# Up-projections of a split-precision transformer kernel with 512 moving columns per matmul, their result read from two half banks by ScalarE and VectorE

## What is computed

```
first block, twice per layer:
  a, b = split(rmsnorm(x, g) @ w_up, 2)          # w_up 1024 x 5632
  x = x + 0.5 * (silu(a) * b) @ w_down           # w_down 2816 x 1024
second block, once per layer:
  a, b = split(dwconv3(rmsnorm(x, g) @ w_up), 2)
  x = x + (silu(a) * b) @ w_down
```

## Time and profile before

| what | value |
|---|---|
| median of 3 runs | 2204.83 us (2196.54 to 2207.15) |
| the profiled execution, its own time | 2198.97 us |
| its span in the trace | 2197.2 us |
| PE busy | 2062.6 us, 94% of the span |
| DVE busy | 1531.2 us, 70% |
| ACT busy | 1044.9 us, 48% |
| mean granted TensorE clock | 0.981 |

### The profile page before, as it was taken

How to read it: one execution, slowest core, us unless ns; L and a number is a source line. 1 busy time by engine, 2 the same in 40 slices (tenths; PEclk the granted TensorE clock), 3 DMA queues, 4 the chain that set the end, 5 groups by cost and what they waited for, 6 DMA issues and landing times.

```text
span 2197.2 us, 39058 instructions
## 1 busy us (share of the span) xinstructions
PE 2062.6 (94%) x15972; PEld 1949.6 (89%) x15972; DVE 1531.2 (70%) x2165; ACT 1044.9 (48%) x1357; POOL 0.2 (0%) x4
## 2 busy tenths in 40 slices
PE   6999999999999899999998999996999997999998
PEld 6998987788999899989778899996788997778998
DVE  5556888977755665568899676556658776647777
ACT  4444453465544444444426654443455554445554
POOL 0000000000000000000000000000000000000000
PEclk9999999999999999999999999998999998999999
DMA  5555443324655345544332255452225543315544
GB/s 224 184 190 199 157 151 115 116 68 136 220 190 186 141 172 189 199 157 171 135 123 85 87 198 200 172 196 77 77 97 186 187 172 120 106 39 191 192 172 153
DMA packets 51153, 336.68 MB, mean 153 GB/s; under 512 B 5688, under 2 KB 5688, under 8 KB 14696
## 3 DMA queue, kind: packets, MB, share of 16 engines
q1 hardware_dynamic: 50616, 332.72, 43.4%
q10 hardware_dynamic: 432, 2.46, 0.3%
HBM read 334.11 MB, written 1.05 MB: 153 GB/s over the span
## 4 chain that ended last, share of the span: by engine, by line
PE 73%; DVE 16%; ACT 7%; DMA 2%; issue 2%; DVEq 0%; ACTq 0%; SPq 0%
PE bank L367 23%; PE bank L368 22%; PE bank L369 22%; DVE lo L1249 5%; ACT hi L828 3%; DVE cv L1466 2%; DMA raw<-in_w 2%; PE bank L393 1%; PE bank L506 1%; PE bank L514 1%; PE bank L501 1%; DVE qn L1392 1%; PE bank L530 1%; DVE p_sb L1445 1%; DVE rstd L1262 0%
## 5 line engine op out<-in xcount | busy, mean ns | idle before, releaser
L1249 DVE TENSOR_TENSOR lo<-raw,hi 128x2048 fp32r<-128x2048 f32 (+1 forms) x344 | 721.0, 2096 | 318.9 <-ACT hi L828 318.7
L828 ACT ACTIVATE hi<-raw 128x2048 fp32r<-128x2048 f32 (+1 forms) x344 | 601.8, 1753 | 163.7 <-PE bank L369 125.9
L367 PE MATMUL bank<-n_hi,hi 128*128 128x256 f32 x2112 | 599.4, 284 | 41.0 <-DVE n_lo L1253 34.0
L368 PE MATMUL bank<-n_lo,hi 128*128 128x256 f32 x2112 | 596.9, 283 | 0.0
L369 PE MATMUL bank<-n_hi,lo 128*128 128x256 f32 x2112 | 596.8, 283 | 0.0
L367 PEld LDWEIGHTS bank<-n_hi,hi 128*128 128x128 f32 x2112 | 400.3, 190 | 43.5 <-issue 29.5
L367 PE MATMUL bank<-h_hi,hi 128*128 128x256 f32 x1296 | 384.0, 296 | 28.5 <-DVE h_lo L1253 27.0
L368 PEld LDWEIGHTS bank<-n_lo,hi 128*128 128x128 f32 x2112 | 400.3, 190 | 0.2
L369 PEld LDWEIGHTS bank<-n_hi,lo 128*128 128x128 f32 x2112 | 400.2, 189 | 0.0
L368 PE MATMUL bank<-h_lo,hi 128*128 128x256 f32 x1296 | 372.3, 287 | 0.0
L369 PE MATMUL bank<-h_hi,lo 128*128 128x256 f32 x1296 | 372.0, 287 | 0.0
(11 more groups left out here) (209 smaller groups left out, 2326.9 us busy)
## 6 DMA issues: line engine op xcount, KB each, us to landing
raw<-in_w SPq DMA_DIRECT2D x282, 1024.0 KB, 4.8
raw<-in_w SPq DMA_DIRECT2D x62, 512.0 KB, 3.8
bv<-in_bv SPq DMA_DIRECT2D x2, 768.0 KB
x<-in_x ACTq DMA_DIRECT2D x1, 1024.0 KB, 5.0
mask_in<-in_const SPq DMA_DIRECT2D x2, 512.0 KB
out_x<-x SPq DMA_DIRECT2D x1, 1024.0 KB, 3.9
const<-in_const ACTq DMA_DIRECT2D x1, 791.5 KB, 12.7
prm_all<-in_prm ACTq DMA_DIRECT2D x1, 588.0 KB, 8.7
```

The lines of the kernel that those rows point to most:

```text
L367: mm(out, w_hi, a_hi, start=start, stop=False, skip_group_check=True)
L368: mm(out, w_hi, a_lo, start=False, stop=False, skip_group_check=True)
L828: fn(hi[:, s, 0:w], raw[:, s, 0:w], ACT.Copy).then_inc(sem["hi"], 1)
L1249: v.tensor_tensor(lo[:, s, 0:w], raw[:, s, 0:w], hi[:, s, 0:w].bitcast(F32), ALU.subtract)\
```

## The change

Input high and low parts become one tensor `n_both`, and the first two matmuls of a product become one with 512 moving columns, its result over a whole bank: columns 0 to 255 get high by high, columns 256 to 511 high by low. The third matmul (low weight by high input, 256 columns) adds to columns 256 to 511. So each j has a bank of its own, four banks for the up chunks (3, 4 and 6, 7), and the down chunks move to banks 5, 0, 1, 2. The two halves must be added: ACT copies both upper halves to `spill_t`, 512 elements (new semaphore `spill`), DVE adds them to the lower halves (`sum_t`), waits for itself, and multiplies by `rstd`. In ACT's order `spill` stands ahead of what used to wait for `up`, which in the loops is behind a `split`. Nothing else of the orders changes; down chunks and all products of the mixers stay as they are.

```diff
+DOWN_BANKS = (5, 0, 1, 2)
+UP_BANKS = ((3, 4), (6, 7))
...
-    n_hi = sb("n_hi", [P, KT, S], F32R, at_u)
-    n_lo = sb("n_lo", [P, KT, S], F32R, at_u + KT * S * 4)
+    n_both = sb("n_both", [P, 2, KT, S], F32R, at_u)
+    n_hi, n_lo = n_both[:, 0, :, :], n_both[:, 1, :, :]
...
+    def up_banks(u):
+        return psum[:, UP_BANKS[u][0]:UP_BANKS[u][1] + 1, :]
...
+        def up_pair(c, u, ready=None, stat_after=None):
+            take("lo")
+            for k in range(KT):
...
                 for j in range(2):
-                    last = mm3(out[:, j * S:(j + 1) * S], tile(hi, c, 2 * k + j), tile(lo, c, 2 * k + j),
-                               a_hi[:, k0 + k, :], a_lo[:, k0 + k, :], start=start and k == 0 and j == 0)
+                    out = bank[UP_BANKS[u][j]]
+                    mm(out[:, :], tile(hi, c, 2 * k + j), n_both[:, :, k, :], start=(k == 0), stop=False,
+                       skip_group_check=True)
+                    last = mm(out[:, S:2 * S], tile(lo, c, 2 * k + j), n_hi[:, k, :], start=False, stop=True,
+                              skip_group_check=True)
             last.then_inc(sem["pe"], 1)
...
+        def spill(u, c):
+            act.wait_ge(sem["pe"], c)
+            fn(spill_t[:, :, :], up_banks(u)[:, :, S:2 * S], ACT.Copy).then_inc(sem["spill"], 1)
...
                 split(cb + 4)
+                spill(0, i * 3 + after0)
                 tap0(0, at(0))
                 hidden(1)
                 split(cb + 5)
                 silu2(0)
                 split(cb + 6)
+                spill(1, i * 3 + (after0 + 1))
                 tap0(1, at(1))
...
-        def up(u, c, out):
-            v.wait_ge(sem["pe"], c)
-            v.tensor_tensor(out, two(bank[u][:, :]), rstd[:, 0, :].unsqueeze(1).broadcast_to([P, 2, S]), ALU.mult)\
+        def up(u, out):
+            take("spill")
+            link(v.tensor_tensor(sum_t[:, :, :], up_banks(u)[:, :, 0:S], spill_t[:, :, :], ALU.add))
+            v.tensor_tensor(out, sum_t[:, :, :], rstd[:, 0, :].unsqueeze(1).broadcast_to([P, 2, S]), ALU.mult)\
                 .then_inc(sem["up"], 1)
```

More of the change, by code:

```diff
@@ L163, in leave @@
             self.n[k] = before.get(k, 0) + v * times
-_FFN_LOOP = dict(hi=3, lo=3, pe=3, slot=3, load0=16, load1=16, load2=16, half=1, up=2, silu=2, prod=2,
+_FFN_LOOP = dict(hi=3, lo=3, pe=3, slot=3, load0=16, load1=16, load2=16, half=1, spill=2, up=2, silu=2, prod=2,
                  hidhi=2, hid=2)
-PER_FFN1 = dict(_FFN_LOOP)
-PER_FFN2 = dict(_FFN_LOOP, tap0=2, conv3=2, link=2)
+PER_FFN1 = dict(_FFN_LOOP, link=2)
+PER_FFN2 = dict(_FFN_LOOP, tap0=2, conv3=2, link=4)
 def _stream(chunks):
@@ L179, in _ffns @@
 def _ffns(n):
-    return dict(half=n * (PAIRS - 1), up=n * JT, silu=n * JT, prod=n * JT, hidhi=n * JT, hid=n * JT,
+    return dict(half=n * (PAIRS - 1), up=n * JT, spill=n * JT, silu=n * JT, prod=n * JT, hidhi=n * JT, hid=n * JT,
                 dpair=3 * n, ssum=n)
@@ L201 @@
              "ythi", "yth", "conv", "mu", "cc", "csq", "cvar", "cstd", "cn", "cs", "cshi", "csh",
-             "mix", "mixhi", "mixh", "link", "out", "nat", "up", "tap0", "dpair", "mask", "conv3", "es", "uhi", "uh", "ghi", "g",
+             "mix", "mixhi", "mixh", "link", "out", "nat", "spill", "up", "tap0", "dpair", "mask", "conv3", "es", "uhi", "uh", "ghi", "g",
              "fhi", "f", "ssum", "rd", "pn", "yc", "yf", "fsq", "fstat", "fstd", "ysum", "ystd", "yn", "mf", "ya")
@@ L297, in build @@
     assert at_u + 28672 <= at_t
-    bank = [nc.alloc_psum_tensor(f"bank{i}", [P, 512], F32) for i in range(8)]
+    psum = nc.alloc_psum_tensor("bank", [P, 8, 512], F32)
+    bank = [psum[:, i, :] for i in range(8)]
     ident = const[:, C["ident"]:C["ident"] + P]
@@ L375, in tile, with pairs @@
             return part[:, c % SLOTS, i * P:i * P + n]
-        def pairs(c, out, k0, nk, a_hi, a_lo, start, ready=None, stat_after=None):
+        def pairs(c, out, k0, nk, a_hi, a_lo, start, ready=None):
             take("lo")
             for k in range(nk):
+                if ready and k % 2 == 0:
+                    take(ready)
+                for j in range(2):
+                    last = mm3(out[:, j * S:(j + 1) * S], tile(hi, c, 2 * k + j), tile(lo, c, 2 * k + j),
+                               a_hi[:, k0 + k, :], a_lo[:, k0 + k, :], start=start and k == 0 and j == 0)
+            last.then_inc(sem["pe"], 1)
+        def up_pair(c, u, ready=None, stat_after=None):
+            take("lo")
+            for k in range(KT):
                 if k == stat_after:
@@ L407, in summed_stat @@
             pe.wait_ge(sem["const"], 16)
[L408 removed]
+            mm(bank[5][:, 0:S], ones, xsq[:, 0, :], start=True, stop=True).then_inc(sem["stat"], 1)
         def down_tile(c, k, m, h_hi, h_lo, start=False):
[L411 removed]
+            return mm3(bank[DOWN_BANKS[m // 2]][:, (m % 2) * S:(m % 2 + 1) * S], tile(hi, c, 8 * k + m),
                        tile(lo, c, 8 * k + m), h_hi[:, k, :], h_lo[:, k, :], start=start)
@@ L443, in two_tiles @@
                 take("up")
-                pairs(cb + 2, bank[0], 0, KT, n_hi, n_lo, True)
+                up_pair(cb + 2, 0)
                 if early:
@@ L447, in two_tiles @@
                 take("up")
-                pairs(cb + (4 if early else 3), bank[1], 0, KT, n_hi, n_lo, True)
+                up_pair(cb + (4 if early else 3), 1)
                 if not early:
                     down(cb + 4, first)
-            pairs(cb, bank[0], 0, KT, n_hi, n_lo, True, ready="h")
-            pairs(cb + 1, bank[1], 0, KT, n_hi, n_lo, True, stat_after=2)
+            up_pair(cb, 0, ready="h")
+            up_pair(cb + 1, 1, stat_after=2)
             cnt.up("sq", 4)
@@ L816, in act_program @@
         cnt = Count(dict(pe=SLOTS))
+        start = {}
         fn = nc.scalar.activation
@@ L866, in scaled_std, with pe_after @@
             take("stat")
-            fn(std[:, 0, :], bank[7][:, 0:S], ACT.Sqrt, scale=1.0 / D, bias=eps).then_inc(sem["std"], 1)
+            fn(std[:, 0, :], bank[5][:, 0:S], ACT.Sqrt, scale=1.0 / D, bias=eps).then_inc(sem["std"], 1)
         def silu(u, gate_of):
             fn(silu_t[:, u, :], gate_of[:, u, 0, :], ACT.Silu).then_inc(sem["silu"], 1)
+        def pe_after(c):
+            return start["pe"] + c + 1
+        def spill(u, c):
+            act.wait_ge(sem["pe"], c)
+            fn(spill_t[:, :, :], up_banks(u)[:, :, S:2 * S], ACT.Copy).then_inc(sem["spill"], 1)
         def silu1(u):
@@ L886, in ffn1 @@
             scaled_std()
+            spill(0, pe_after(cb))
             silu1(0)
@@ L890, in ffn1 @@
             hidden(0)
+            spill(1, pe_after(cb + 1))
             silu1(1)
@@ L903, in ffn1 @@
                 split(cb + 6)
+                spill(1, i * 3 + (after0 + 2))
                 silu1(1)
@@ L910, in ffn1 @@
             split(c + 2)
+            spill(0, pe_after(c))
             silu1(0)
@@ L913, in ffn1 @@
             split(c + 3)
+            spill(1, pe_after(c + 1))
             silu1(1)
@@ L1005, in layer1 @@
         def layer1():
+            start["pe"] = cnt.at("pe")
             take("prm")
```

40 lines of the change are left out of this document (21 added, 19 removed).

## The result

| | before | changed |
|---|---|---|
| median of the runs, us | 2203.52 (4 runs) | 2224.86 (2222.76 to 2226.78, 4 runs) |
| profiled execution / its span, us | 2198.97 / 2197.2 | 2226.37 / 2224.6 |
| mean granted clock of that span | 0.981 | 0.975 |

A forecast was written before the change was run, and what follows sets the result against it. It took PE, busy 94% of the span, as the bound, with DVE and ACT deciding at starts, ends and in the second block's loop. -3.3 + 15.6 = +12.3 us on 2198.97 gave 2211.3, as median 2217 us, range 2200 to 2230.

The forecast's parts named there:

- 10.9 ns a product: Up-projections on PE: a product falls from 356.1 to 345.2 ns, -23.0 us in all if nothing else holds PE.
- Rival (d): Up-projection matmuls: cost is per column, a 512-column one takes 237.4 ns beside a 256-column one; 2228 us, chance 0.12.
- the -3.3 forecast there: First block's four feed-forward parts: cheaper products less new waits at starts and ends, -3.3 us for the four.
- One of the forecast's own signs of being wrong: First block's feed-forward (`ffn1`): an up chunk above 5.6 us would show the forecast wrong.
- 17.08 us a round, so PE's gain there is nothing: Second block's 18 loop rounds: DVE and ACT set 17.08 us a round, against 17.09 before and 16.74 of PE.
- The circle: Second block's loop: DVE and ACT wait on each other in a closed chain without PE, 17.08 us a round.
- a second register link: DVE between the convolution's halves in the second block's loop: half of 0.11 us extra, twice a round.
- the branch: ACT in the second block's loop: the loop's branch adds 0.15 us, 0.48 instead of 0.33 between two starts.
- rival (b): Part of the gain arrives: mixed stream saves more, 2204 us, or links and branches cost less, 2211; chance 0.19.
- +7.8 a part: Second block: each part's last down chunk starts 7.8 us later, +15.6 us for both parts.
- I price that difference at 0: Second block's end: slower clock after the longer 6.3 us wait counted as 0, upper bound some 3 us a part.
- my case: The main forecast for the whole kernel, 2217 us, own range 2209 to 2226, chance 0.46.

The follow-up runs named there:

- e2: Against the changed kernel: three 256-column matmuls per product again, into the two half banks, with copy and sum kept; 2227.01 us, ratio to before 1.0120.
- e3: Against the changed kernel: wide matmuls kept, copy and sum removed, so up-projections' low-part products are left out of the result; 2193.59 us, ratio to before 0.9958.
- e4: Against the changed kernel: the change only in the first block's four feed-forward parts, second block as before; 2205.43 us, ratio to before 1.0014.
- e5: Against the changed kernel: both 512-column matmuls of a k step first, then both 256-column ones; 2218.83 us, ratio to before 1.0067.
- e1: Against the changed kernel: input laid out so the 512 moving columns are one contiguous run; 2220.82 us, ratio to before 1.0085.

## Why the prediction was right, and where it was not

**Direction and mechanism: right.** It said that the gain per product is eaten by a longer chain at starts and ends, where PE already waits, and most of all in the second block. e2 and e3 show just that, and e4 that the second block holds most of the loss. The sizes of these waits were near: 4.38 us for the second tile (4.9 forecast), the first down chunk 4.3 us later (4.6), the `last_lo` wait 1.2 in the first block (1.5) and 5.2 and 4.9 in the second (6.3).

**"10.9 ns a product": more than twice what came.** It is 4.9 by the rounds. The step that failed is taking 226.5 ns from the value projection and setting it beside 118.7 from the old up chunk: steps of two streams do not carry over into a mixed third. Rival (d) asked just this, with all 10.9 lost. Over the 1408 products of the first block the miss is 8.4 us, and it accounts for most of the distance between the -3.3 forecast there and the +6.1 in the profile. It is also the largest miss in the total, which came out 9.0 us over the forecast difference. One of the forecast's own signs of being wrong came with it: an up chunk of `ffn1` takes (16.93 - 5.70) / 2 = 5.62 us, above 5.6. The Trainium skill's "TensorE: Matmul & The Clock Gate", section "Back-to-back issue gap", gives, in its formula for the isolated gap, about 2.5 ns a matmul beside its columns, so by it a join would save 2.5; the runs show 4.9, nearer to the page than to the 10.9 of my rows; the most that any run showed is 7.4 (e5).

**"17.08 us a round, so PE's gain there is nothing": wrong in the sum, near in its effect.** The circle is 16.85. Of the 0.23 us, 0.11 is the price set on a second register link, which does not show (the half round with the link fits without it); 0.08 is the branch (0.40 us between `silu` and the weight copy at 1789.42, where 0.48 was taken from the earlier trace rows), and the rest rounding in the terms. Its price lay in rival (b). But with PE at 16.93, not 16.74, circle and PE are nearly equal, and 0.16 us a round is all that arrives: 1.4 us a part. PE was not seen waiting before every down chunk, as the forecast had it.

**"+7.8 a part" in the second block.** At the last down chunk of the first part it is 5.4: 1.3 from the faster rounds and 1.1 from the shorter end wait. The first part is 5.6 us longer and the second 9.8. That the sum is 15.3 against 15.6 is luck: chain and rounds cost less than forecast, and some 4 us of clock, which I had priced at 0, fill the gap, nearly all of them in the second part; the windows behind its waits have 0.72 and 0.66.

**"I price that difference at 0": wrong, by some 5 us in the parts.** I looked mainly at the end of a part, where a low stretch was there already, and bounded it by 3 us a part. New stretches came behind new or longer waits at the starts, and the one behind the wait for the first down chunk's low weight was not hidden. Whether the clock also cost time in stages that the change does not touch is not shown: the 6.1 us there are within what single executions scatter by. The time ends at 2224.9, inside my case's own range of 2209 to 2226, but by two errors of one sign, product and clock, and one of the other, the second block's circle and end wait, which were set too long.

## What to carry to other kernels

Joining matmuls saves only what the mixed stream saves: time the stream itself, in a round, before you multiply by a thousand products. A longer evacuation chain costs nothing in the middle of a loop where its engine has room, and its full length at each start and end where PE already waits, so split such a change by place and keep it only where no one waits. What PE loses at a start is not made good in rounds in which PE works without a gap, except by what the rounds themselves became shorter.

## What was not expected of the hardware

Each 0.001 of mean granted clock goes with 1.6 to 2.1 us of this kernel's time, within runs of one program. With wide matmuls on top of the same chain the mean clock was 0.004 lower in the changed kernel and 0.001 lower in e1 than in e2, four runs each, so whether they lower it is open. And 512-column matmuls take 226.5 ns in one stream and 233 in another with the same clock granted, with no cause found; reordering the same instructions moved a product by 2.3 ns.
